# Two projections of block two start on the residual without root and shift, which are put in when their sums are read out

## The reference

```python
mod = silu(c) @ w_mod + b_mod                       # 6 vectors of D
sh1, sc1, g1, sh2, sc2, g2 = split(mod, 6)
h = rmsnorm_2(x, attn_norm_g) * (1 + sc1) + sh1
proj = h @ w_in                                     # q of the window attention: columns 0 to 1023
...
x = x + g1 * (mix @ w_out)
h = rmsnorm_2(x, mlp_norm_g) * (1 + sc2) + sh2
u = relu(h @ w_ff1)
x = x + g2 * ((u * u) @ w_ff2)
```

## Time and profile before

| | |
|---|---|
| median of 3 runs | 2143.18 us (2142.56 to 2143.39) |
| the profiled execution | 2144.41 us |
| its span in the profile | 2142.1 us |
| PE busy | 2115.5 us (99%) |
| DVE busy | 1488.8 us (70%) |
| ACT busy | 1058.3 us (49%) |
| granted PE clock, mean | 0.998 |

### The profile page before, as it was taken

The page is one execution under the profiler, slowest core; times in us unless marked ns, Lnnn a source line. Parts: engine busy times, 40 slices in busy tenths (PEclk is TensorE's granted clock), DMA queues, the critical chain, the costliest instruction groups (busy, mean ns, idle before and its releaser), DMA issues.

```text
span 2142.1 us, 29202 instructions
## 1 busy us (share of the span) xinstructions
PE 2115.5 (99%) x11416; PEld 1829.1 (85%) x11416; DVE 1488.8 (70%) x1972; ACT 1058.3 (49%) x1515; POOL 46.2 (2%) x48
## 2 busy tenths in 40 slices
PE   8999999999999999999999999999999999999998
PEld 7888888888888788888888898888888888888886
DVE  6867665788998787989755666566554565555655
ACT  6654555554444344444455665555443444334443
POOL 3200000000000000000000000000000000000000
PEclk9999999999999999999999999999999999999999
DMA  8787323788988998889864534455555555555553
GB/s 325 259 299 266 120 99 114 275 312 323 341 333 319 319 346 331 334 320 336 282 215 156 203 105 171 161 183 207 196 188 189 194 190 189 193 194 195 181 185 127
DMA packets 73240, 496.81 MB, mean 232 GB/s; under 512 B 8474, under 2 KB 8650, under 8 KB 16528
## 3 DMA queue, kind: packets, MB, share of 16 engines
q1 hardware_dynamic: 69984, 481.85, 63.4%
q0 software_dynamic: 2544, 12.44, 1.6%
q10 hardware_dynamic: 576, 0.66, 0.1%
HBM read 492.75 MB, written 2.16 MB: 231 GB/s over the span
## 4 chain that ended last, share of the span: by engine, by line
PE 93%; ACT 3%; DVE 2%; DMA 2%; issue 1%; POOL 0%; DVEq 0%; SPq 0%; ACTq 0%
PE region L1017 40%; PE region L961 30%; PE region L965 15%; PE bank L1086 2%; PE bank L1049 2%; ACT m_WHI L1369 1%; DMA m_RAW<-in_ffn_w_out 1%; PE region L1006 1%; PE bank L1058 1%; PE bank L1000 1%; DVE m_WLO L1715 1%; DMA m_RAW<-in_nsa_w_in 1%; ACT m_HL L1557 0%; PE bank L1110 0%; PE region L1007 0%
## 5 line engine op out<-in xcount | busy, mean ns | idle before, releaser
L1715 DVE TENSOR_TENSOR m_WLO<-m_RAW,m_WHI 128x1024 fp32r<-128x1024 f32 (+3 forms) x732 | 881.4, 1217 | 524.7 <-ACT m_WHI L1369 500.1
L1369 ACT ACTIVATE m_WHI<-m_RAW 128x1024 fp32r<-128x1024 f32 (+3 forms) x732 | 756.7, 1044 | 718.6 <-PE region L1017 352.0
L1017 PE MATMUL region<-m_WHI,m_HL 128*128 128x512 f32 x1152 | 361.4, 395 | 2.7 <-issue 1.7
L961 PE MATMUL region<-m_HL,m_WHI 128*128 128x512 f32 x1472 | 358.8, 393 | 1.3 <-DVE m_kcT L1627 1.3
L961 PE MATMUL region<-m_H,m_WHI 128*128 128x512 f32 x1376 | 328.7, 391 | 0.0
L961 PEld LDWEIGHTS region<-m_HL,m_WHI 128*128 128x128 f32 x1472 | 270.0, 189 | 53.4 <-DVE m_kcT L1627 1.6
L961 PEld LDWEIGHTS region<-m_H,m_WHI 128*128 128x128 f32 x1376 | 252.8, 188 | 48.9
L1017 PEld LDWEIGHTS region<-m_WHI,m_HL 128*128 128x128 f32 x1152 | 212.6, 188 | 45.5 <-issue 3.3
L1756 DVE CUSTOM_DVE_ANT_0 m_RAW<-m_RAW,m_CROW,m_consts 128x2048 f32<-128x2048 f32 x96 | 225.1, 2344 | 0.0
L1017 PE MATMUL region<-m_WLO,m_HL 128*128 128x512 f32 x576 | 224.7, 390 | 0.0
L1017 PE MATMUL region<-m_WHI,m_HIDH 128*128 128x512 f32 x512 | 199.2, 389 | 0.0
(11 more groups left out here) (306 smaller groups left out, 1798.5 us busy)
## 6 DMA issues: line engine op xcount, KB each, us to landing
m_RAW<-in_w_ff SPq DMA_DIRECT2D x124, 1024.0 KB, 4.8
m_RAW<-in_w_mod SPq DMA_DIRECT2D x96, 1024.0 KB, 6.5
m_RAW<-in_ffn_w_in SPq DMA_DIRECT2D x88, 1024.0 KB, 6.1
m_RAW<-in_ffn_w_out SPq DMA_DIRECT2D x44, 1024.0 KB, 7.0
m_RAW<-in_nsa_w_in SPq DMA_DIRECT2D x36, 1024.0 KB, 5.0
m_RAW<-in_nsa_w_out SPq DMA_DIRECT2D x16, 1024.0 KB, 4.8
m_RAW<-in_w_out SPq DMA_DIRECT2D x16, 1024.0 KB, 4.8
m_RAW<-in_w_in SPq DMA_DIRECT2D x8, 1024.0 KB, 6.9
```

The lines of the kernel that those rows point to most:

```text
L961: mm = e.matmul(region[s["reg"]][:, b, :], hi[:, i, c:c + 128], both[:, k + a + i, :, :].rearrange("p a s -> p (a s)"), start=k + a + i == ...
L1017: mm = e.matmul(o, lhs, rhs, start=start and i == 0, stop=fin and i == 2, skip_group_check=True)
L1369: e.activation(WHI[u % 4][:, 0:(z - a) * ncol], raw[:, a * ncol:z * ncol], ACT.Copy).then_inc(a_hi, 1)
L1715: e.tensor_tensor(WLO[u % 4][:, 0:m], raw[:, a * ncol:z * ncol], WHI[u % 4][:, 0:m].bitcast(F32), ALU.subtract).then_inc(v_lo, 1)
```

## The change

What it does:

- **u tiles.** For the slabs qa 0, 1 and relu 0, 1 the input is no longer the normed h4 or h6 but u4 or u6: XGT itself, split into HI and LO in the same HL tiles (step `usplit`, two tiles at a time, ACT then DVE). Tiles 0 to 11 are split beside the last chunk of down1z 12 or out2 12, tiles 12 to 15 when the last rows have been turned (`xturn`, now whole).
- **The read-out.** For qa 0 and 1 step `qfix` multiplies by the root (DVE) and adds shift times weights (ACT). For relu 0 and 1 step `ufix` does the same, then relu and square; it and `hid` of both slabs stand behind the read-out of relu 1 and behind the last `norm`.
- **norm** is now four steps of four tiles, each put when qa1 or relu1 has used the four u tiles that it overwrites.
- **The boundary.** The last slab ends as the others do. No matmuls of ones. `stat` stands right behind the sums, `rowcast` and `xturn` come from the side queue.
- **Shift times weights.** The shift goes to HBM (`shift`), comes back as a row in CROW (`shiftrow`) once all of mod is done, and 8 steps `shiftsum` on DVE each load 1 MB (a new input w_first, 128 columns of w_in or w_ff1 with the features in the same order as the stored shift) and sum it against CROW. The credit per chunk goes from 0.75 to 0.8.
- **Gates** are stored in 128 pieces of 64 bytes; w_mod and b_mod are laid out so that mod's columns come out in that order.

The diff, cut to its core:

```diff
-    sl_qa = [slab("qa", i, W, 0, KT, 256 * i, 256, WIDE, "h4", per=4) for i in range(2)]
+    sl_qa = [slab("qa", i, W, 0, KT, 256 * i, 256, WIDE, "u4", per=4) for i in range(2)]
...
+    def make_norm(x):
+        put("norm", x, normed[x])
+        normed[x] += 1
+
+    def norms():
+        for x, r in (("h4", 2), ("h6", 3)):
+            if have["row"] == r and normed[x] < behind[x]:
+                make_norm(x)
...
+    def boundary(x, r):
+
+        put("stat", r)
+        side.extend([None, None, ("rowcast", r), ("xturn", x, 12), None] + [lambda m=m: make_u("u" + x[1], m) for m in (12, 14)])
...
+        elif s["x"] == "u4":
+            put("qfix", m0)
+        elif s["x"] == "u6" and m0 == 1:
+            while normed["h6"] < 4:
+                make_norm("h6")
+            for i in range(2):
+                put("ufix", s["i"] - 1 + i)
+                put("hid", s["i"] - 1 + i)
...
+            if s["kind"] in ("down1z", "out2") and s["arg"] == 12 and last and kk:
+                for m in (4 * kk - 4, 4 * kk - 2):
+                    make_u("u4" if s["kind"] == "down1z" else "u6", m)
...
-    st["gemv"] = 0.75
+    st["gemv"] = 0.8
...
+            elif name == "usplit":
+                x, m = arg
+                w.wait_ge(b_out[4 + m % 4 // 2], filled(("xturn", "h" + x[1], m // 4 * 4), 4 + m % 4 // 2))
+                w.wait_ge(p_part, tiles_free(x, m))
+                e.activation(HI[:, m:m + 2, :], XGT[:, m:m + 2, :], ACT.Copy).then_inc(a_u, 1)
...
+                x, c = arg
+                w.wait_ge(v_ht, c + (1 if x == "h4" else 5))
+                w.wait_ge(p_part, tiles_used(x, c))
+                for i in range(4):
+                    m = 4 * c + i
+                    sh = mod[:, m:m + 1] if x == "h4" else mod[:, 48 + m:49 + m]
+                    e.activation(HI[:, m, :], HT[c % 2][:, i, :], ACT.Identity, bias=sh).then_inc(a_norm, 1)
...
+            elif name == "ufix":
+                s = SLABS[arg[0]]
+                i, h = s["arg"], s["hid"]
+                sa = quarter_of(SA, h)
+                w.wait_ge(r_out[s["reg"]], s["free"][1])
+                w.wait_ge(b_out[6], filled(("rowcast", 3), 6))
+                e.tensor_tensor(sa, sa, by_token(rstd, 2), ALU.mult).then_inc(v_ufix, 1)
+                w.wait_ge(a_ufix, i + 1)
+                w.wait_ge(a_norm, 32)
+                w.wait_ge(v_norm, 32)
+                e.scalar_tensor_tensor(quarter_of(HT, h), sa, 0.0, sa, ALU.max, ALU.mult).then_inc(v_hid, 1)
+            elif name == "shiftsum":
+                i, = arg
+                raw, landing, value = raw_of("s", i)
+                w.wait_ge(landing, value)
+                w.wait_ge(l_shiftrow, 16 * (i // 4 + 1))
+                e.tensor_tensor_reduce(out=raw[:, :], in0=raw[:, :], in1=CROW[:, :], scale=0.125 if i < 4 else 1.0, scalar=0.0,
+                                       op0=ALU.mult, op1=ALU.add, accum_out=shifted[:, i:i + 1]).then_inc(v_shift, 1)
...
-                e.dma_start(bass.AP(tensor=dst.tensor, offset=dst.offset, ap=[[1, 128], [128, 16]]),
-                            mod[:, 16 * p:16 * p + 16], allow_slow_non_contiguous=True).then_inc(l_gate[p // 3], 16)
+                e.dma_start(gate_rows[i].rearrange("(p j) -> p j", p=128), mod[:, 16 * p:16 * p + 16]).then_inc(l_gate[i], 16)
```

More of the change, by code:

```diff
@@ L262, in make_plan @@
     side, later, every = deque(), [], []
-    st = dict(split=0, cursor=0, rate=1, due=0.0, parts=0, held=[], owed=0, gemv=0.0, credit=0.0)
-    have = {"h1": 0, "h2": 0, "h3": 0, "h5": 0, "row": 0, "rstd": False}
+    st = dict(split=0, cursor=0, rate=1, due=0.0, parts=0, held=[], gemv=0.0, credit=0.0)
+    have = {"h1": 0, "h2": 0, "h3": 0, "h5": 0, "u4": 0, "u6": 0, "row": 0, "rstd": False}
     unscaled = []
-    normed = {"h4": 0, "h6": 0}
+    normed, behind = {"h4": 0, "h6": 0}, {"h4": 0, "h6": 0}
     flushing = []
-    gemvs = deque((p, j) for p in range(6) for j in range(16))
+    gemvs = deque(("g", (p, j)) for p in range(6) for j in range(16))
+    for r in range(2):
+        gemvs.extend([("row", r), None] + [("s", 4 * r + i) for i in range(4)])
     def unit(*u):
@@ L332, in next_gemv, with make_u @@
             return
-        p, j = gemvs.popleft()
-        load("g", (p, j))
-        put("gemv", p, j)
[L336 to L348, removed]
+        g = gemvs.popleft()
+        if g is None:
+            return
+        what, i = g
+        if what == "row":
+            put("shiftrow", i)
+            return
+        load(what, i)
+        if what == "s":
+            put("shiftsum", i)
+            return
+        p, j = i
+        put("gemv", p, j)
+        if j == 15:
+            put({0: "shift", 1: "factors", 2: "gate"}[p % 3], p // 3)
+    def make_u(x, m):
+        assert have[x] == m
+        put("usplit", x, m)
+        have[x] = m + 2
+    def make_norm(x):
[5 more added lines that the diff above has]
+                make_norm(x)
     def x_ready(s, k):
@@ L356, in x_ready @@
         if x in normed:
[L357 to L364, removed]
+            while normed[x] <= k // 4:
+                make_norm(x)
+        elif x in ("h2", "h3", "h5", "u4", "u6"):
             while have[x] <= k:
@@ L370, in row_half @@
         put("half", s["i"], h)
[L371 to L378, removed]
-    def finish_by_halves(s):
[L382 to L401, removed]
-        unit("rowcast", 2 if which == "h4" else 3)
-        idle(6)
-        st["owed"] = 2
+        put("sqhalf", 3, s["arg"], h)
+    def finish_by_halves(s):
+        for h in range(2):
+            row_half(s, h)
+            put("stat4", h)
+            put("store", h)
+            if h == 0:
+                for n, kk in st["held"]:
+                    put("mm2", n, kk)
+                st["held"].clear()
+    def boundary(x, r):
+        put("stat", r)
+        side.extend([None, None, ("rowcast", r), ("xturn", x, 12), None] + [lambda m=m: make_u("u" + x[1], m) for m in (12, 14)])
     def finish_slab(s):
@@ L484, in run_chunk @@
         flush_later()
+        if s["x"] in ("u4", "u6") and s["arg"] == 1:
+            behind["h" + s["x"][1]] = k // 4 + 1
         if last:
@@ L487, in run_chunk @@
         split()
-        if last and s["kind"] in ("glu", "relu"):
+        if last and s["kind"] in ("glu", "relu") and s["x"] != "u6":
             put("hid", s["i"])
+        norms()
         tick()
@@ L1125, in tensor_program @@
                 sum_of_squares(*arg)
-            elif name == "ones":
-                n, turn_of_bank = arg
-                w.wait_ge(b_out[7], turn_of_bank)
-                for _ in range(n):
-                    e.matmul(bank[7][:, 0:128], ones[:, :], ones[:, :], start=True, stop=True)
             elif name == "mm2":
```

182 lines of the change are left out of this document (114 added, 68 removed).

## The result

The change makes the kernel slower, about as forecast: 2159.72 us (median of 4 runs, 2159.07 to 2163.59) against 2143.28 before, measured beside it; ratio 1.0079, 95% interval 1.0067 to 1.0091, so +16.9 us (+14.4 to +19.5). The forecast was 2161 with 2149 to 2168. The profiled execution took 2159.17 us with a span of 2157.3, 15.2 more than before's.

What follows compares the result with a forecast made beforehand. PE bounds the kernel, busy 99% of the span. Gates -2.5, first boundary +7.6, second boundary +7.3 and clock +5.1 sum to +17.5 us, so 2161 us against the runs' median, range 2149 to 2168.

Steps and rivals of the forecast that it cites:

- Gates: Gate stores at 700 to 740 us: 64-byte pieces win back all PE lacks there, -2.5 us; bounds all or nothing.
- Shift sums: Block one: eight multiply-and-sums, 19 us more on DVE, stay hidden, 0 us; DVE 90.7 to some 93 of 100 us.
- First boundary: From down1z's end to qa2: PE waits 5.3 us at the rowcast and from 34.0 to 40.3 ahead of ka; +7.6 us.
- The walk: Step-by-step timing of ACT's and DVE's queues behind both boundaries, dependent steps following 0.04 to 0.1 us after the one before.
- Second boundary: From zero at 1416.14 to relu2's end: PE waits 5.4 us at the rowcast and 6.3 us inside relu2; +7.3 us.
- The wait inside relu2: PE wants the split of relu2 k12-15 at 45.0, done at 51.3 behind norm 3 and relu's fixes: 6.3 us.
- Clock: Half clock behind PE's waits, 1.7 us each at both rowcasts and relu2's last part, +5.1 us; vanishes behind ka's wait.
- The bounds: Whole forecast: no clock loss and half the lag caught up, +8 (2151); clock twice as dear and sums felt, +26 (2169).
- engines keep up: Rival at both boundaries: ACT and DVE clear queues faster, only rowcasts and relu's chain cost; about 2147 to 2149, chance 0.14.

Runs made afterwards that it cites:

- ones_fit: Changed kernel with 22 matmuls of ones ahead of each rowcast, to fit the wait; ratio 1.0066 to the kernel before.
- fix_later: Changed kernel with the split of relu2 k12-15 ahead of norm 3 and of both slabs' fixes; ratio 1.0054 to the kernel before.
- row_later: Changed kernel with the rowcast two ticks later at both boundaries, plus a guard on ACT ahead of qa's read-outs; ratio 1.0054 to the kernel before.
- product_ahead: Changed kernel with each norm's product on DVE ahead of the weight split, plus the guard on ACT ahead of qa's read-outs; ratio 1.0030 to the kernel before.
- combo_later_sums: Changed kernel with norm products ahead of splits, relu2's last split earlier, u splits behind the sums, rowcast two ticks later; ratio 0.9976 to the kernel before.
- ones_row: Changed kernel with 36 matmuls of ones ahead of both rowcasts; ratio 1.0091 to the kernel before.
- sums_first: Changed kernel with u4/u6 tiles 4 to 10 split behind the last sums and the root's step; ratio 1.0064 to the kernel before.
- chains_apart: combo_later_sums with both slabs of relu's fix stepped together and qa's fixes behind ka k0 to 7; 2134.79 us, ratio 0.9955 to the kernel before.

## Why the prediction was right

**Gates, -2.5.** As forecast: PE loses nothing at 700 to 740 us, in the changed kernel and with this part alone.

**Shift sums, 0.** As forecast, both by taking them out and by PE, which is never idle from 600 to 1100 us. That DVE would go from 90.7 to some 93 of 100 us was high by one: 92.1.

**First boundary, +7.6 and 1.7 for the clock.** A is +9.3. The rowcast came at 13.27 (forecast 13.3) after 5.13 us of wait (5.3), ka at 42.5 (40.3 plus 1.7) after 5.8 us (6.3). The walk through DVE's and ACT's order was good to a few tenths; where it was out, at the norms, which end on ACT some 2 us later than in the walk, it was the clock that I had charged by itself: in ones_fit norms 0, 1 and 2 end at 22.7, 30.1 and 37.4 us (walk: 22.9, 30.3, 37.7).

**Second boundary, +7.3 and 3.4 for the clock.** B is +10.4. The rowcast came at 11.96 (12.0) after 5.22 us (5.4); relu2 at 38.3 (36.7 plus 1.7). The wait inside relu2 was 4.2 and not 6.3 us: PE came there 48.5 us behind zero instead of 45.0 (1.6 us from relu2's later start, 1.9 from half clock in its first parts) and got its split at 52.7 instead of 51.3; its place and its cause are as forecast, shown by fix_later.

**Clock, +5.1.** About right in sum, too simple in kind. The three terms of 1.7 us measure 2.5 and 1.6 (ones_fit) and 1.6 (relu2's last part, read from row_later), 5.7 us in all. But PE worked at half clock at five places, not three: behind both rowcasts, at ka, at relu2's start and at its last part. At ka and at relu2's start another wait follows and takes it up, as I had held for ka.

**The bounds.** Some of the sums around the forecast don't come out. No clock loss and half of the 14.9 us caught up gives +5 us, not +8. The clock twice as dear and 5 us for the sums gives +27.6, not +26. The rival "engines keep up" begins at 2146 us, not 2147. The measured 2159.72 is in the range either way. That both boundaries came out within 0.3 us is in part luck: A differs by up to 0.7 us between profiles of the same steps, and the clock behind a wait of 2 to 4 us goes both ways (last section).

**Why the norm chains cost.** Here the working had the right size by walking the given order, and I took that order's cost as a load on ACT and DVE. product_ahead shows that 9.0 us of ACT at the first boundary were no load but a wait for a product that stood one place too late (10.1 us of waits became 1.1), and that A falls by 7.3 us without them. The rival "engines keep up" was right in that sense: they can, in another order, and then (combo_later_sums) the boundaries cost what they did before. Of the idea itself, to start on the bare residual, 4.8 us (A -1.4, B -3.4) can be had, 5.8 by the two ratios (0.9955 against 0.9982 for the gates alone).

**Where row_later missed.** I had held that a wait of PE ahead of late queues only moves, and gave 1.5 us. The order was worth 1.7 us, near that; the other 4.1 us of A and B were the clock, which I had left out of the expectation.

## What to carry to other kernels

Taking a dependency off the busiest engine's path paid here only once the strict order of the other engines let the new work run in their gaps. Look first for a short product that stands behind an operation which itself waits, and for two engines that take turns on one item while a second item is ready. When a wait of the matmul engine changes its length, look at the granted clock behind it before anything is said about the order: the clock was two thirds of what moving the rowcast won. Matmuls of ones in a wait gave back the clock where they ended with it, and gained nothing where they ran 2.7 us over; take the time of one from a row first.

## What the runs showed of the hardware

One and the same wait of 1.9 us at 68 us in block one was followed by half clock in 6 of 14 profiles and by full clock in 8, among them the changed kernel's. Before:

```profile
66.00:80.00 14.00, 12.11 (x70) 10.84 (x69) 13.65 (x9) 6.72 (x8) 9.21 (x5) 0.88 0.73 245
```

and the changed kernel:

```profile
66.00:80.00 14.00, 12.10 (x77) 10.67 (x76) 13.96 (x10) 7.57 (x8) 9.23 (x5) 1.00 0.72 249
```

Of 14 us at a mean of 0.88 some 1.7 us of work are lost. Zero of the first boundary came 4.48 us earlier in the changed kernel, 2.53 of them from the gate; the rest is about this much. So the span of one execution can be 2 us off for no reason in the kernel, and differences of that size between single profiles were read here from A and B.

Behind block one, every wait of PE between 4.2 and 6.1 us in these profiles (22 of them) had a granted clock of 0.50 behind it. Of the 18 waits between 1.8 and 3.8 us, 14 had and 4 had not, and one and the same wait goes both ways: the 2.6 us ahead of relu2 were followed by half clock in the changed kernel, ones_row and ones_fit and by full clock in sums_first, the 1.8 us at the second rowcast by half clock in chains_apart and by full clock in combo_later_sums. So a difference of up to 1.6 us between two of these profiles can be the clock alone.
